# Expert weights as plain fp32 in column groups, instead of split in two fp32r parts

## The chip, the cores and the metric

The kernel runs on one core of one Trainium2 chip. The metric is the device time of one execution in microseconds (us); lower is better. A core has TensorE (PE, whose weight loads are listed as PEld), VectorE (DVE), ScalarE (ACT), GpSimd (POOL) and SyncE (SP, which here issues the loads). TensorE can be used as one array of 128 columns, or in column groups of 64 or 32, each with weights of its own and writing to its own partitions of PSUM.

## The reference

One step of a diffusion backbone of width 1024 with 128 context tokens and 512 latent tokens. After the attention part comes a layer of experts, on which the change works:

```
def expert_choice_ffn(h, w_router, w_gate, w_up, w_down):
    cap = CAPACITY_FACTOR * n // N_EXPERTS          # 64 latent, 16 context tokens for each of 16 experts
    aff = softmax(h @ w_router)
    gates, idx = top_k(swapaxes(aff, 1, 2), cap)
    xe = h[idx]
    a = einsum('becd,edf->becf', xe, w_gate)        # 1024 x 1024 per expert, fp32
    u = einsum('becd,edf->becf', xe, w_up)
    ye = einsum('becf,efd->becd', silu(a) * u, w_down) * gates
    return zeros.at[idx].add(ye)                    # added to the chosen tokens' rows
...
x = x + gate2 * expert_choice_ffn(h, *moe_w)        # then a last RMSNorm
```

Context tokens and latent tokens choose separately, with the same weights. All inputs are fp32.

## The kernel before

The first 600 us are projections and attention; their code doesn't change. Then the layer of experts runs in four groups of four experts. An expert has three weights (gate, up, down; `BLOCK_ORDER` interleaves them so that a hidden row is ready when "down" needs it), and each weight comes in 8 halves of 128 x 1024 fp32, 512 KB: 96 halves a group, 384 in all. SP issues one DMA a half into one of `ESLOT` = 12 slots, once PE has counted (`s_half`) that the slot's last half is used.

A half is split before use: ScalarE writes `w_hi` (the weight rounded to fp32r, L1608), VectorE the rest, `raw_lo` or `extra_lo` (L1972), four halves ahead (`LEAD`). The tokens are split in the same way (`xe_hi`, `xe_lo`; hidden rows `ht2_hi`, `ht2_lo`). The tokens are the stationary operand: 80 columns, 64 latent and 16 context. `half_product` (L1238) makes, for each side of 512 columns, three fp32r products (hi x hi, hi x lo, lo x hi; L1246 to L1248). The result stands on partitions 0 to 79 of two banks.

Between the halves PE does three more things. `turn_hidden` (L1230) transposes the hidden rows of an expert (8 transposes), at the third and fourth half of the next gate block. `find_rows` (L1208, L1210) looks up the chosen tokens' row numbers and gates for four experts, once a group: plain fp32 products with 64 columns (latents) and 16 columns (context, from partition 64). `gather` and `gather_context` (L1193, L1177) pick the next group's tokens by products with a 0/1 matrix, in the last "down" block of a group. `spare` (L1237) and `keep_warm` (L1156) are fillers. `gate_spread` (L1130, L1132) puts the second gate's row onto the partitions ahead of the experts.

After "down", VectorE multiplies by gate and modulation (`y_g`), and GpSimd adds the 80 rows of 4 KB to `x1_dram` by an indirect DMA (`scatter`, L2433), one after the other. The last expert isn't scattered: its eight "down" halves run one side first (all of side 0, then the end of side 1), VectorE adds `y_g` to gathered rows, and two indirect DMAs write them to the outputs (L2449, L2451).

Each engine's work is an order written out by hand; semaphores alone tie them. A plain fp32 product appears in the trace as two records (and two weight loads), an fp32r product as one.

Of the kernel before, what the change touches and what calls it, by code (L numbers as in the profile page):

```python
# [51 lines left out]
ESLOT, LEAD = 12, 4  # L52
# [137 lines left out]
T_ID, T_IOTA, T_SLAT, T_SCTX, T_EPS, T_NH, T_ONES = 0, 128, 192, 193, 194, 195, 196  # L190
T_KEPT = 200
# [5 lines left out]
def table_of_constants():  # L197
# [9 lines left out]
    t[:, T_ONES] = 1.0  # L207

# [18 lines left out]
def build(nc, x_prompt, x_sample, cache_attn_k, cache_attn_v, cache_diff_k, cache_diff_v, c, c_ctx,  # L227
# [5 lines left out]
    with ctx:  # L233
# [25 lines left out]
        gate_e = sb("gate_e", [P, EG])  # L259
        rows_e = sb("rows_e", [P, NE], U32)  # L260
# [104 lines left out]
        extra_lo = [at("extra_lo0", 129024, [P, 2, HALF], F32R), at("extra_lo1", 88064, [P, 2, HALF], F32R)]  # L365
        ht2_hi = at("ht2_hi", 96256, [P, KD, EROWS], F32R)
        ht2_lo = at("ht2_lo", 100352, [P, KD, EROWS], F32R)
        h_act = at("h_act", 104448, [P, 2, NW])
        y_g = at("y_g", 108544, [P, 2, D])
        sel_c = at("sel_c", 151040, [P, EG * CAPC], F32R)  # L370
        sel_g = at("sel_g", 137216, [P, NTL, EG * CAPL], F32R)
        x_lat = at("x_lat", 141312, [P, 2, EG * CAPL])
# [8 lines left out]
        x1_dram = nc.dram_tensor("x1_dram", [TOK, D], F32).ap()  # L381
# [31 lines left out]
        s_gb1 = sem("s_gb1"); s_gb2 = sem("s_gb2"); s_xr = sem("s_xr")  # L413
# [6 lines left out]
        s_selg = sem("s_selg"); s_g = sem("s_g"); s_xeh = sem("s_xeh"); s_xel = sem("s_xel")  # L420
# [7 lines left out]
        s_out = sem("s_out"); s_kout = sem("s_kout"); s_htf = sem("s_htf"); s_kn = sem("s_kn"); s_xet = sem("s_xet")  # L428
        s_q2 = [sem("s_q2a"), sem("s_q2b")]; s_yme = sem("s_yme"); s_xech = sem("s_xech"); 
# [69 lines left out]
        def expert_half(h):  # L499
            s = h % ESLOT  # L500
            return raw_half(raw, DENSE_HALVES + s) if s < 2 * NRAW else extra[(s - 2 * NRAW) // 2][:, s % 2, :]

        def expert_lo_half(h):
            s = h % ESLOT
            return raw_half(raw_lo, DENSE_HALVES + s) if s < 2 * NRAW else extra_lo[(s - 2 * NRAW) // 2][:, s % 2, :]
# [60 lines left out]

        def latent_slots(xe, k):
            return xe[:, k, :].rearrange("p (e s) -> p e s", s=EROWS)[:, :, 0:CAPL]

        def by_expert(x):  # L570
            return x.rearrange("p (e s) -> p e s", s=CAPL)

        def context_slots(xe):
            return xe.rearrange("p k (e s) -> p (k e) s", s=EROWS)[:, :, CAPL:EROWS]

        def hidden_bank(f):
            return bank(6 + f).rearrange("p (k c) -> p k c", c=P)[:, :, 0:EROWS]
# [35 lines left out]
        def _(sp):  # L613
# [58 lines left out]
            def body(i, first):  # L672
                for h in range(GH):
# [4 lines left out]
                    if first and h == 8:  # L678
                        for t in range(NT):
                            sp.wait_ge(s_x1, t + 1)  # L680
                            sp.dma_start(x1_dram[t * P:(t + 1) * P, :], x_r[:, t, :]).then_inc(s_x1out, 16)
                    if not first or h >= ESLOT:
# [4 lines left out]
                    elif h == 2 * NRAW:  # L687
                        sp.wait_ge(s_lgt, 2)
                    elif h == 2 * NRAW + 2:
                        sp.wait_ge(s_xl, NT)  # L690
# [6 lines left out]
            sp.wait_ge(s_scat, 16 * (NE - 1))  # L697
# [12 lines left out]
        def _(pe):  # L710
# [411 lines left out]
            def gate_spread(r):  # L1122

                pe.wait_ge(s_grow, r + 1)
                if r == 0:
                    pe.wait_ge(s_gb2, 16)
                b = 6 + r
                for v in range(2):
# [3 lines left out]
                pe.matmul(bank(b), ones_m[0:1, :], gate2[0:1, r * NW:(r + 1) * NW], start=False, stop=True)\  # L1132
                  .then_inc(s_post, 1)
# [64 lines left out]
            def find_rows(i, first, last):  # L1198
# [4 lines left out]
                if not first:  # L1203
                    pe.wait_ge(s_h2l, i * 8)
# [1280 lines left out]
```

## Time and profile before

| | us |
|---|---|
| median of 3 runs | 1240.54 |
| lowest, highest | 1237.38, 1240.97 |
| span of the profiled execution | 1235.4 (its time around the span is not given) |
| busy PE, weight loads | 1191.7, 859.5 |
| busy DVE, ACT, POOL | 913.9, 721.9, 181.6 |
| bytes moved | 291.62 MB, mean 236 GB/s |

The profile's page gives busy time by engine, the chain that ended last and the costliest lines; the stage tables and timelines are answers of the trace to a question about a stretch. Durations of matmuls overlap: what a matmul costs is the distance to the next one's start, not its own length. The layer of experts lies between about 613 and 1221 us, 384 x 512 KB = 201 MB of the bytes.

### The profile page before, as it was taken

Reading aid. Unit: us, or ns where it says so; the run is one execution under the profiler, and the core shown is the slowest. Engines: PE = TensorE matmul, PEld = TensorE weight load, DVE = VectorE, ACT = ScalarE, POOL = GpSimd, SP = SyncE. Lnnn points to the kernel's source line nnn. Section 1 sums busy time; section 2 is a strip of 40 time slices with the busy share of each in tenths; the row PEclk is TensorE's granted clock in tenths of the full one; section 3 lists DMA queues with packets and bytes.
Section 4 is the critical chain, followed back from the end, with each engine's and each line's share of the span. In section 5 each row is a group of like instructions: output and inputs, shape, how many; then the busy total and the mean of one; then the engine's idle time right before and its main releaser. Section 6 shows DMA issues by size and latency. Waiting matters only on the chain.

```text
span 1235.4 us, 17478 instructions
## 1 busy us (share of the span) xinstructions
PE 1191.7 (96%) x6111; PEld 859.5 (70%) x6111; DVE 913.9 (74%) x1145; ACT 721.9 (58%) x1029; POOL 181.6 (15%) x154
## 2 busy tenths in 40 slices
PE   6999999999999999999899999999999999999994
PEld 4778877788777777778476667666676666766662
DVE  3673658899682322444778999899997999979995
ACT  4432357777641230223567776788766777667774
POOL 1344330000000000100400111110114110111220
PEclk9999999999999999999889999999999999999997
DMA  9932250110424444472559998899989999799995
GB/s 361 332 134 69 71 117 23 44 31 14 184 68 171 136 136 145 155 265 70 220 187 330 387 376 306 314 373 386 384 268 321 369 387 385 257 335 366 380 392 196
DMA packets 110862, 291.62 MB, mean 236 GB/s; under 512 B 29265, under 2 KB 30498, under 8 KB 110274
## 3 DMA queue, kind: packets, MB, share of 16 engines
q1 hardware_dynamic: 106576, 273.16, 60.8%
q0 software_dynamic: 3792, 12.86, 4.2%
q10 hardware_dynamic: 418, 4.63, 1.0%
q8 instruction: 43, 0.70, 0.2%
q14 instruction: 33, 0.27, 0.1%
HBM read 269.64 MB, written 15.73 MB: 231 GB/s over the span
## 4 chain that ended last, share of the span: by engine, by line
PE 87%; DVE 6%; ACT 3%; issue 2%; DMA 1%; ACTq 0%; POOL 0%; DVEq 0%; POOLq 0%
PE ps L1246 14%; PE ps L1247 14%; PE ps L1248 14%; PE ps L742 9%; PE ps L743 8%; PE ps L744 8%; PE ps L968 2%; PE ps L952 2%; DVE neg_max L1881 2%; PE ps L1193 1%; PE ps L991 1%; PE ps L1194 1%; PE ps L987 1%; DVE q_lo_t L1873 1%; PE ps L764 1%
## 5 line engine op out<-in xcount | busy, mean ns | idle before, releaser
L1972 DVE TENSOR_TENSOR raw_lo<-raw,w_hi 128x1024 fp32r<-128x1024 f32 x256 | 304.6, 1218 | 44.9 <-ACT w_hi L1608 33.4
L1608 ACT ACTIVATE w_hi<-raw 128x1024 fp32r<-128x1024 f32 x252 | 264.8, 1060 | 79.7 <-PE ps L1248 79.7
L1246 PE MATMUL ps<-w_hi,xe_hi 128*80 128x512 f32 x512 | 204.6, 400 | 0.0
L1248 PE MATMUL ps<-w_hi,xe_lo 128*80 128x512 f32 x512 | 203.3, 397 | 0.0
L2433 POOL DMA_INDIRECT x_dram<-y_g,rows_e x15 | 93.6, 6238 | 499.6 <-DVE y_g L2201 499.6
L1972 DVE TENSOR_TENSOR extra_lo<-extra,w_hi 128x1024 fp32r<-128x1024 f32 x128 | 152.6, 1219 | 7.0 <-ACT w_hi L1608 5.9
L1608 ACT ACTIVATE w_hi<-extra 128x1024 fp32r<-128x1024 f32 x128 | 135.9, 1064 | 36.6 <-PE ps L1248 36.6
L742 PE MATMUL ps<-w_hi,ht 128*128 128x512 f32 (+1 forms) x320 | 124.8, 390 | 0.0
L744 PE MATMUL ps<-w_hi,ht 128*128 128x512 f32 (+1 forms) x320 | 121.7, 380 | 0.0
L743 PE MATMUL ps<-raw_lo,ht 128*128 128x512 f32 (+1 forms) x320 | 121.7, 380 | 0.0
L522 DVE TENSOR_TENSOR raw_lo<-raw,w_hi 128x1024 fp32r<-128x1024 f32 x48 | 57.6, 1225 | 78.9 <-ACT w_hi L517 78.3
L517 ACT ACTIVATE w_hi<-raw 128x1024 fp32r<-128x1024 f32 x48 | 48.8, 1053 | 114.2 <-DMA raw<-in_w_in_dram 66.3
L1247 PE MATMUL ps<-raw_lo,xe_hi 128*80 128x512 f32 x288 | 114.1, 396 | 0.0
L1248 PEld LDWEIGHTS ps<-w_hi,xe_lo 128*80 128x80 f32 x512 | 76.5, 149 | 43.5 <-issue 1.4
L1246 PEld LDWEIGHTS ps<-w_hi,xe_hi 128*80 128x80 f32 x512 | 76.7, 150 | 40.8 <-issue 1.4
L1246 PE MATMUL ps<-w_hi,ht_hi 128*80 128x512 f32 x256 | 100.9, 394 | 0.3 <-DVE ht_lo L2190 0.2
L1248 PE MATMUL ps<-w_hi,ht_lo 128*80 128x512 f32 x256 | 100.6, 393 | 0.0
L1247 PE MATMUL ps<-extra_lo,xe_hi 128*80 128x512 f32 x224 | 89.0, 397 | 0.0
L1247 PE MATMUL ps<-raw_lo,ht_hi 128*80 128x512 f32 x224 | 88.2, 394 | 0.0
L742 PEld LDWEIGHTS ps<-w_hi,ht 128*128 128x128 f32 x320 | 60.1, 188 | 16.6 <-issue 5.2
L744 PEld LDWEIGHTS ps<-w_hi,ht 128*128 128x128 f32 x320 | 60.0, 187 | 12.9
L743 PEld LDWEIGHTS ps<-raw_lo,ht 128*128 128x128 f32 x320 | 60.1, 188 | 11.2
(328 smaller groups left out, 2056.4 us busy)
## 6 DMA issues: line engine op xcount, KB each, us to landing
raw<-in_w_exp_down_dram SPq DMA_DIRECT2D x112, 512.0 KB, 6.4
raw<-in_w_exp_gate_dram SPq DMA_DIRECT2D x80, 512.0 KB, 5.4
extra<-in_w_exp_up_dram SPq DMA_DIRECT2D x64, 512.0 KB, 5.6
raw<-in_w_exp_up_dram SPq DMA_DIRECT2D x64, 512.0 KB, 5.5
extra<-in_w_exp_gate_dram SPq DMA_DIRECT2D x48, 512.0 KB, 5.2
raw<-in_w_in_dram SPq DMA_DIRECT2D x16, 1024.0 KB, 5.7
raw<-in_w_mod_dram SPq DMA_DIRECT2D x12, 1024.0 KB, 7.1
raw<-in_w_mod_dram SPq DMA_DIRECT2D x16, 512.0 KB, 11.0
```

The lines of the kernel that those rows point to most:

```text
L517: act.activation(w_hi[:, n % NHL, :], raw_half(raw, h), ACT.Copy).then_inc(s_hi, 1)
L522: dve.tensor_tensor(raw_half(raw_lo, h), raw_half(raw, h), w_hi[:, n % NHL, :].bitcast(F32), ALU.subtract)\
L742: pe.matmul(b, stat_hi(k, tt), hi[:, kk, :], start=first, stop=False)
L743: pe.matmul(b, stat_hi(k, tt), lo[:, kk, :], start=False, stop=False)
L744: mm = pe.matmul(b, stat_lo(k, tt), hi[:, kk, :], start=False, stop=last)
L952: mm = pe.matmul(bank(bb, 0, n), q[:, m % 4, t * P:(t + 1) * P], keys_t[:, x, c0:c0 + n], start=(part == 0), stop=(part == 1))
L1246: pe.matmul(b, stat_hi, hi[:, cols], start=(k == 0), stop=False)
L1247: pe.matmul(b, stat_hi, lo[:, cols], start=False, stop=False)
L1248: mm = pe.matmul(b, stat_lo, hi[:, cols], start=False, stop=(k == KD - 1))
L1608: act.activation(w_hi[:, (DENSE_SPLITS + h) % NHL, :], expert_half(h), ACT.Copy)\
L1972: dve.tensor_tensor(expert_lo_half(h), expert_half(h), w_hi[:, (DENSE_SPLITS + h) % NHL, :].bitcast(F32), ALU.subtract).then_inc(s_lo, 1)
L2433: pool.indirect_dma_start(x1_dram[:, :], bass.IndirectOffsetOnAxis(ap=rows_e[0:EROWS, n:n + 1], axis=0), y_g[0:EROWS, n % 2, :], None, com ...
```

## The change

- The weights aren't split. A half is used as it landed, as plain fp32; the tokens too (`xe_l` latents, `xe_c` context padded to 32, `ht2_l`, `ht2_c`). The split instructions of ScalarE and VectorE in this stage go, and `half_product` waits for the slot's DMA.
- `half_product` makes two products of 64 stationary columns (latents) over 512 columns each, in column groups 0 to 63 and 64 to 127 of one bank, and four of 32 (context) over 256 columns each in four groups of the next. A side of the result thus stands on other partitions: latents in half rows, context in quarter rows.
- The last expert's eight halves (`side_product`) put, for each side, latents on partitions 0 to 63 and context on 64 to 95.
- The hidden rows are turned by four transposes (`turn_latents`) and two (`turn_context`) of 128 columns.
- `find_rows` puts each table on both 64-partition groups and on four 32-partition groups; `gate_spread` makes the gate's rows in those layouts as well; row numbers are doubled or quadrupled.
- `scatter` issues two indirect DMAs for an expert, 128 half rows of 2 KB and 128 quarter rows of 1 KB; the padding goes to 16 spare rows behind `x1_dram`, which SP fills with one more store.
- Sixteen slots: the room of `w_hi` becomes `extra_ring`.

```
-ESLOT, LEAD = 12, 4
+ESLOT = 16
...
-        xe_hi = at("xe_hi", 61440, [P, KD, EG * EROWS], F32R)
-        xe_lo = at("xe_lo", 74752, [P, KD, EG * EROWS], F32R)
+        xe_l = at("xe_l", 61440, [P, KD, EG * CAPL])
+        xe_c = at("xe_c", 69632, [P, KD, EG, 32])
...
-                def half_product(h, banks, stat_hi, stat_lo, k, sides=(0, 1)):
-                    pe.wait_ge(s_lo, i * GH + DENSE_SPLITS + h + 1)
-                    hi, lo = w_hi[:, (DENSE_SPLITS + h) % NHL, :], expert_lo_half(h)
-                    for f in sides:
-                        cols = slice(f * NW, (f + 1) * NW)
-                        b = bank(banks + f, rows=slice(0, EROWS))
-                        pe.matmul(b, stat_hi, hi[:, cols], start=(k == 0), stop=False)
-                        pe.matmul(b, stat_hi, lo[:, cols], start=False, stop=False)
-                        mm = pe.matmul(b, stat_lo, hi[:, cols], start=False, stop=(k == KD - 1))
-                    if 1 in sides:
+                def half_product(h, banks, latents, context, k):
+
+                    pe.wait_ge(s_slot[h % ESLOT], expert_raw(h, i))
+                    w, flags = expert_half(h), {"start": k == 0, "stop": k == KD - 1}
+                    for f in range(2):
+                        pe.matmul(bank(banks, rows=slice(64 * f, 64 * f + 64)), latents, w[:, f * NW:(f + 1) * NW], **flags)
+                    for q in range(4):
+                        mm = pe.matmul(bank(banks + 1, 0, 256, slice(32 * q, 32 * q + 32)), context,
+                                       w[:, 256 * q:256 * q + 256], **flags)
+                    mm.then_inc(s_half, 1)
+
+                def side_product(h, f, latents, context, k):
+
+                    pe.wait_ge(s_slot[h % ESLOT], expert_raw(h, i))
+                    w, flags = expert_half(h)[:, f * NW:(f + 1) * NW], {"start": k == 0, "stop": k == KD - 1}
+                    pe.matmul(bank(4 + f, rows=slice(0, CAPL)), latents, w, **flags)
+                    mm = pe.matmul(bank(4 + f, rows=slice(64, 96)), context, w, **flags)
+                    if f:
                         mm.then_inc(s_half, 1)
                     elif k == KD - 1:
                         mm.then_inc(s_front, 1)
...
                for e in range(EG):
                     cols = (e * (NE + 1), (e + 1) * (NE + 1))
                     for t in range(NTL):
+                        for f in range(2):
+                            pe.matmul(bank(6, *cols, slice(64 * f, 64 * f + 64)),
+                                      sel_g[:, t, e * CAPL:(e + 1) * CAPL].bitcast(F32), aff_n[:, t, :],
+                                      start=(t == 0), stop=(t == NTL - 1))
+                    cols = ((EG + e) * (NE + 1), (EG + e + 1) * (NE + 1))
+                    for g in range(4):
+                        mm = pe.matmul(bank(6, *cols, slice(32 * g, 32 * g + 32)), sel_c[:, e, :].bitcast(F32),
+                                       aff_n[:, NTL, :], start=True, stop=True)
...
-            def expert_lo(h, i):
-                dve.wait_ge(s_hi, i * GH + DENSE_SPLITS + h + 1)
-                dve.tensor_tensor(expert_lo_half(h), expert_half(h),
-                                  w_hi[:, (DENSE_SPLITS + h) % NHL, :].bitcast(F32), ALU.subtract).then_inc(s_lo, 1)
...
-                pool.indirect_dma_start(x1_dram[:, :], bass.IndirectOffsetOnAxis(ap=rows_e[0:EROWS, n:n + 1], axis=0),
-                                        y_g[0:EROWS, n % 2, :], None, compute_op=ALU.add).then_inc(s_scat, 16)
+                pool.indirect_dma_start(x1_halves[:, :], bass.IndirectOffsetOnAxis(ap=rows_l[:, n:n + 1], axis=0),
+                                        y_l[:, n % 2, :], None, compute_op=ALU.add).then_inc(s_scat, 16)
+                pool.indirect_dma_start(x1_quarters[:, :], bass.IndirectOffsetOnAxis(ap=rows_x[:, n:n + 1], axis=0),
+                                        y_c[:, n % 2, :], None, compute_op=ALU.add).then_inc(s_scat, 16)
```

TensorE's order before, in any block of the stage, here "down" (`ht_hi`, `ht_lo` are the hidden rows; 80x512 is stationary columns by streamed columns):

```order
L1246 MATMUL ps<-w_hi,ht_hi 80x512
L1247 MATMUL ps<-raw_lo,ht_hi 80x512
L1248 MATMUL ps<-w_hi,ht_lo 80x512
L1246 MATMUL ps<-w_hi,ht_hi 80x512
L1247 MATMUL ps<-extra_lo_133,ht_hi 80x512
L1248 MATMUL ps<-w_hi,ht_lo 80x512
```

And after the change, in the gate block of the second expert, with the transposes of the first expert's hidden rows (`h_l` latents, `h_c` context):

```order
L1278 MATMUL ps<-raw,xe_l 64x512 x2
L1280 MATMUL ps<-raw,xe_c 32x256 x4
L1257 MATMUL ps<-tab,h_l 128x128 x4
L1278 MATMUL ps<-raw,xe_l 64x512 x2
L1280 MATMUL ps<-raw,xe_c 32x256 x4
L1265 MATMUL ps<-tab,h_c 128x128 x2
L1278 MATMUL ps<-raw,xe_l 64x512 x2
L1280 MATMUL ps<-raw,xe_c 32x256 x4
```

Six products of one size a half have become two of 64 columns and four of 32, in turn; the transposes stand between halves as before. In the last expert's last block, after the change (L1271 are fillers):

```order
L1271 MATMUL ps<-sel_g 128x256 x9
L1257 MATMUL ps<-tab,h_l 128x128 x4
L1265 MATMUL ps<-tab,h_c 128x128 x2
L1271 MATMUL ps<-sel_g 128x256 x11
L1288 MATMUL ps<-extra_ring,ht_l 64x512
L1289 MATMUL ps<-extra_ring,ht_c 32x512
L1288 MATMUL ps<-extra_ring,ht_l 64x512
L1289 MATMUL ps<-extra_ring,ht_c 32x512
```

There a product of 64 columns and one of 32, both over 512 columns, follow each other 16 times.

## Rows read from the trace of the kernel before

**Rows 1.** The page's first lines: span, busy time by engine, share, instructions.

```profile
span 1235.4 us, 17478 instructions
PE 1191.7 (96%) x6111; PEld 859.5 (70%) x6111; DVE 913.9 (74%) x1145; ACT 721.9 (58%) x1029; POOL 181.6 (15%) x154
```

**Rows 2.** The chain that ended last, by line.

```profile
PE ps L1246 14%; PE ps L1247 14%; PE ps L1248 14%; PE ps L742 9%; PE ps L743 8%; PE ps L744 8%; PE ps L968 2%; PE ps L952 2%; DVE neg_max L1881 2%; PE ps L1193 1%; PE ps L991 1%; PE ps L1194 1%; PE ps L987 1%; DVE q_lo_t L1873 1%; PE ps L764 1%
```

**Rows 3.** Busy time by stage (stretch, length, engines, clock, DMA share, GB/s).

```profile
core 0: us, PE busy (x) PEld busy (x) DVE busy (x) ACT busy (x) POOL busy (x), PEclk, DMA share, GB/s
606.20:623.20 17.00, 16.77 (x58) 12.21 (x59) 11.81 (x29) 2.90 (x6) 2.32 (x2) 0.50 0.18 62
...
943.90:947.70 3.80, 3.80 (x12) 2.28 (x12) 1.37 (x4) 0.89 (x1) 2.50 (x1) 0.55 0.67 184
...
1150.00:1203.00 53.00, 53.00 (x236) 34.09 (x235) 48.89 (x45) 41.89 (x43) 14.05 (x3) 1.00 1.02 389
```

**Rows 4.** PE timeline, first matmuls of two blocks (start, length, idle before in brackets).

```profile
700.23 0.39 PE L1246 MATMUL ps<-w_hi,ht_hi 128*80 128x512 f32 x1
...
711.31 0.39 PE L1246 MATMUL ps<-w_hi,xe_hi 128*80 128x512 f32 x1
```

**Rows 5.** Chain in order of time: two look-ups of rows (start, length).

```profile
793.08 0.57 PE ps L1208 x8
...
941.21 0.57 PE ps L1208 x8
```

**Rows 6.** PE timeline, four column groups between 128-column products.

```profile
38.63 0.39 PE L896 MATMUL ps<-w_hi,ht 128*128 128x512 f32 x1
38.95 1.90 PE L774 MATMUL ps<-raw,vec_t 128*2 128x512 f32 x16
40.77 0.50 PE L894 MATMUL ps<-w_hi,ht 128*128 128x512 f32 x1
41.11 0.39 PE L895 MATMUL ps<-raw_first_lo,ht 128*128 128x512 f32 x1
```

**Rows 7.** PE timeline of two 64-column groups, and their line's durations.

```profile
191.63 1.52 PE L987 MATMUL ps<-p_t,va_n 128*64 128x256 f32 x12
193.07 0.77 PE L968 MATMUL ps<-tab,probs 128*128 128x128 f32 x5
...
L987 PE MATMUL ps<-p_t,va_n x192: 379/379/431, 191.6 to 265.4; 128*64 128x256 f32 x192
```

**Rows 8.** PE timeline of the look-up, 64 and 16 columns in turn, and L1208's durations.

```profile
643.43 0.64 PE L1208 MATMUL ps<-aff_n,sel_g 128*64 128x17 f32 x8
644.00 0.22 PE L1210 MATMUL ps<-aff_n,sel_c 128*16 128x17 f32 x2
644.15 0.64 PE L1208 MATMUL ps<-aff_n,sel_g 128*64 128x17 f32 x8
...
L1208 PE MATMUL ps<-aff_n,sel_g x128: 210/210/231, 643.4 to 1093.5; 128*64 128x17 f32 x128
```

**Rows 9.** PE timeline, transposes of the hidden rows.

```profile
692.76 0.44 PE L1230 MATMUL ps<-tab,h_act 80*128 80x80 f32 x4
693.00 0.44 PE L1246 MATMUL ps<-w_hi,xe_hi 128*80 128x512 f32 x1
```

**Rows 10.** PE timeline ahead of the experts.

```profile
603.75 0.73 PE L1156 MATMUL ps<-xn_hi 128*128 128x512 f32 x2
606.43 1.98 PE L1130 MATMUL ps<-mod_keep,tab 128*64 128x512 f32 x4 [1.95 <-ACT mod_keep L1590]
...
613.20 0.71 PE L1167 MATMUL ps<-tab,pos_t 16*128 16x16 f32 x5
```

**Rows 11.** The scatter's line: durations, first and last start.

```profile
L2433 POOL DMA_INDIRECT x_dram<-y_g,rows_e x15: 5537/5537/13485, 681.6 to 1194.5; - x15
```

**Rows 12.** Chain in order of time, the end.

```profile
1220.63 0.75 DVE y_g L2261
...
1227.04 0.30 POOL out_dram L2449
```

More of the change, by code:

```diff
@@ L190 @@
 T_ID, T_IOTA, T_SLAT, T_SCTX, T_EPS, T_NH, T_ONES = 0, 128, 192, 193, 194, 195, 196
+T_OFFL, T_OFFC = 197, 198
 T_KEPT = 200
@@ L207, in table_of_constants @@
     t[:, T_ONES] = 1.0
+    t[:, T_OFFL] = p // 64
+    t[:, T_OFFC] = np.where(p % 32 < CAPC, p // 32, 4 * (TOK + p % 32 - CAPC) + p // 32)
     for v in range(2):
@@ L1131, in gate_spread @@
                               start=True, stop=False)
-                pe.matmul(bank(b), ones_m[0:1, :], gate2[0:1, r * NW:(r + 1) * NW], start=False, stop=True)\
-                  .then_inc(s_post, 1)
+                bias = gate2[0:1, r * NW:(r + 1) * NW]
+                pe.matmul(bank(b), ones_m[0:1, :], bias, start=False, stop=True)
+                if r == 0:
+                    pe.wait_ge(s_affc, 1)
+                half = slice(64 * r, 64 * r + 64)
+                o = T_SB - T_KEPT
+                pe.matmul(bank(4, rows=half), tab2[:, o:o + 64], mod_keep[:, r, :], start=True, stop=False)
+                pe.matmul(bank(4, rows=half), ones_m[0:1, half], bias, start=False, stop=True)
+                for g in range(2):
+                    rows, cols = slice(64 * r + 32 * g, 64 * r + 32 * g + 32), slice(256 * g, 256 * g + 256)
+                    pe.matmul(bank(1, 0, 256, rows), tab2[:, o + P:o + P + 32], mod_keep[:, r, cols], start=True, stop=False)
+                    mm = pe.matmul(bank(1, 0, 256, rows), ones_m[0:1, rows], bias[:, cols], start=False, stop=True)
+                mm.then_inc(s_post, 1)
             for n in range(NT, 2 * NT):
@@ L1635, in body @@
                                 gathered(0, q, True)
-                        if not last or KD * n + k + LEAD < GH:
-                            expert_hi(KD * n + k + LEAD, i)
                         if before == "g" and k == 1:
@@ L1640, in body @@
                             silu(e1, 1)
-                        if before == "u" and kind == "g" and k in (4, 5):
-                            hidden_hi(e1, k - 4)
+                        if before == "u" and kind == "g" and k == 4:
+                            latents_turned(e1)
                         if (kind, e) == ("d", EG - 1):
@@ L2208, in body @@
                         h = KD * n + k
-                        if first and n == 0:
-                            for q in GATHERS_READ.get(k, ()):
-                                gathered(0, q, True)
                         if before == "u" and k == 0:
@@ L2217, in body @@
                             output(e1)
-                        if not last or h + LEAD < GH:
-                            expert_lo(h + LEAD, i)
                         if before == "d" and k == 1 and (n or not first) and not early:
                             output(e1)
-                        if before == "u" and kind == "g" and k in (4, 5):
-                            hidden_lo(e1, k - 4)
+                        if before == "u" and kind == "g" and k == 5:
+                            context_turned(e1)
                         if h == 12:
```

328 lines of the change are left out of this document (163 added, 165 removed).

## The prediction, written before the change was run

> **What bounds the kernel now.** I read the page's busy shares first. TensorE (PE) is busy 96% of a span of 1235.4 us [rows 1]. A busy PE need not be PE at its peak, so the chain of waits comes next: the three matmul lines of the expert stage, L1246 to L1248, hold 42% of it, and VectorE 6% [rows 2]. The stage table then says what runs beside them: in a full stretch of experts PE has no gap, VectorE is at 48.89 of 53 us, ScalarE at 41.89, the DMA share is 1.02 and 389 GB/s move at full clock [rows 3]. So PE sets the pace of the 384 weight halves (16 experts, 3 matrices, 8 halves of 512 KB), the splits on ScalarE and VectorE fit under it, and the transfers have little room: 524,288 B at 389 GB/s are 1.35 us a half. The PE timeline gives the pace: a block of 8 halves starts at 700.23 and the next at 711.31, so a half costs 11.08 / 8 = 1.385 us for 6 matmuls, 0.231 each [rows 4]. A whole group of four experts, from one look-up of rows to the next, takes 941.21 - 793.08 = 148.1 us [rows 5].
>
> **The change, part by part: the pace of a half.** The splits go away, which frees VectorE and ScalarE but nothing on the path. What counts is PE's new work for a half: two plain fp32 products over 512 columns in column groups of 64, then four over 256 columns in groups of 32. The trace has plain fp32 products in groups. A plain fp32 product leaves two records. L774's 16 records are 8 products in four groups, four rounds; they start at 38.95 and the next line at 40.77 [rows 6]. So a round over 512 columns is under (40.77 - 38.95) / 4 = 0.455 us, and 0.43 once the end is taken off (below). L987's 12 records are six rounds of two 64-wide groups over 256 columns: 193.07 - 191.63 = 1.44 us, 0.216 a round plus what the ends cost [rows 7]. Groups of one size thus run side by side. Streams of a half: 2 x 0.43 + 2 x 0.216 = 1.29 us, 0.09 less than now.
>
> Against it stands the end of each such run. From the last fp32r matmul at 38.63 to L774 at 38.95 pass 0.32 us where the pitch is 0.231: 0.09 lost. L774's own 1.82 us are 4 x 0.427 (two passes over 512 columns need 1024 / 2.4 GHz) and 0.11 lost, and the L894 behind shows 0.50 where its neighbours show 0.39: its 128-column load is exposed, 0.11 [rows 6]. L987 loses 1.44 - 6 x 0.216 - 0.05 = 0.10, where 0.05 is its own first load (maximum 431 ns against a median of 379) [rows 7]. The look-up of rows changes from 64-wide to 16-wide groups and back for each expert: a record more costs (0.64 - 0.21) / 7 = 0.06, but 8 records and the change take 0.57 and 2 records and the change back 0.15, which leaves 0.09 and up to 0.10 or 0.13 (the second run's records may overlap) [rows 8]. The two groups lie on different columns, and no wait is named between them. The transposes L1230 between 128-wide matmuls take 0.24 + 0.05 for four, no such loss [rows 9]. So what costs 0.1 us is a change of group size, not of line or data. The new half changes size twice: 2 x 0.10, and the first load of each run, 0.05 for 64 columns [rows 7] and about 0.02 for 32 (an estimate between nothing and that). Half: 1.29 + 0.20 + 0.07 = 1.56; I take 1.57, as four groups start a little apart. Ends: 1.47 (0.09 a change, loads hidden) and 1.71 (0.13 a change, loads of 0.05 and 0.11).
>
> The Trainium skill, TensorEngine Tiling (Array Packing), Key Properties, says that a change of tiling mode, and not one of tile alone, drains the array; it gives no price. By it both changes of a half are drained, also where 64- and 32-wide groups share columns, which no row here has.
>
> 376 halves run so (all but the last eight): 376 x (1.57 - 1.385) = +69.6 us; ends +32 and +122.
>
> **The last eight halves.** They go side by side: for each half and side one 64-wide product over 512 columns, then one 32-wide, on other columns but of another size, as in rows 8. Each pays both changes: 0.86 + 0.10 + 0.02 + 0.86 + 0.11 + 0.05 = 1.98 us (rounded up by a hundredth, less for an even start), 16 times, 31.7 us for 8 x 1.385 = 11.1: +20.6. Ends +19 and +23.
>
> **Transposes, gathers, look-up.** Before, eight transposes of an expert cost 2 x 0.29 [rows 9]. Now they are four and two of 128 columns instead of 80, 0.24 / 4 x 128 / 80 = 0.10 each, and each of the two runs breaks in between 32- and 64-wide groups: one change more, with a load of 0.11. 6 x 0.10 + 2 x 0.21 = 1.02, less 0.58: +0.44, 16 times, +7. The gathers that stand between halves add one change each in the same way: about 19 of them at 0.21, +4. The look-up puts its 64-wide records in pairs of groups, so 16 take the time of 8, and its four 32-wide ones run beside each other: nothing, but 0.8 for the extra table of the last group. Sum +11.8; ends +7 and +16.
>
> **The gate rows before the experts.** gate_spread runs twice and gets two 64-wide and four 32-wide products more each: 2 x 0.86 + 2 x 0.43 + changes, 3.2 us at full clock, 5.6 to 6.2 at half. The first stands before an idle of 1.95 us, the second before fillers that wait for the positions at 613.20 [rows 10]. In this stretch the clock is at its lower level, 1.2 GHz, from 606.2 to 623.2 [rows 3], after PE had idled. If the new work fills that idle, the gathers behind run at 2.4 GHz and up to 4 us come back; if not, up to 7 are lost. I take +2. Two fills with zeros on VectorE stand there too, about 1 us beside the same wait.
>
> **Scatter and tail.** Two scatters of 128 pieces for one of 80 rows: GpSimd takes 5.5 us now (median) [rows 11]; 2 x 5.5 x 128 / 80 = 18 us, and an expert lasts over 35: hidden. After the last y at 1220.63 the chain goes through a tile of x_f whose output ends just before GpSimd's scatter at 1227.04 [rows 12]. With ScalarE and VectorE free that tile is out long before; the last rows themselves could be scattered about 2 us earlier: -2. The sixteen slots and the transfers cost nothing at 1.57 us a half (334 GB/s): the DMA share falls.
>
> **Sum.** 1235.4 + 69.6 + 20.6 + 11.8 + 2 - 2 = 1337.4 us of span. The profile gives no time of its execution beside the span; the runs' median, 1240.54, lies 5.1 above it (the fastest run 2.0), so 1342.5 us.
>
> **Rivals.** (a) The changes of size inside a half are free, since both sizes use the same columns or the loads slip in ahead. Then a half is 1.29. In a group PE takes 96 x 1.29 = 124 us and the transfers 96 x 1.35 = 130; the gathers give the transfers some 10 us more and sixteen slots carry it over, so PE leads: 376 x -0.095 = -36, the last block 8 x (1.72 - 1.385) = +2.7, transposes 16 x (0.64 - 0.58) = +1, the look-up +1, tail -2: 1202 of span, 1207 us. If the transfers lead, -13 instead, 1230. For it: no row changes size on the same columns. Against it: every change in the trace costs the same 0.1, also between columns that don't touch. It wins from a change below 0.04 us on. Chance 9%.
> (b) Only one of the two directions costs. Half 1.43: +17, last block +18, rest +11: 1286. Against it: rows 6 and 8 show both directions. 5%.
> (c) The groups don't run side by side with 64 and 32 wide weights: 2 x 0.86 + 4 x 0.43 = 3.44 us, +790 us, 2030. Rows 6 and 7 speak against it; 1%. The Trainium skill, TensorE: Matmul & The Clock Gate, Part 3, measured 2.38 times from three 32-wide groups, not 3; by that the streams would be 1.29 / 0.79 = 1.63, a half 1.90 and the time about 1467. The four groups of rows 6 don't show it.
> (d) The change costs more than I say: clock drops like the one behind the look-up (a mean of 0.55 over 3.8 us, 1.7 lost [rows 3]) come at other places too, because the array streams 82% of a half instead of 92%, or loads are exposed at each round. 1380 and more, 6%. Against it: the full stretch of experts in rows 3 stands at 1.00, transposes included.
>
> **Numbers.** My case 79%, with its own range of 1298 to 1375. The range for 8 in 10 is 1293 to 1382: it takes in the one-change case only at its edge. What can be told from no change is 0.3%, 3.7 us. Faster 9% (a), same 1%, slower 90%.
>
> **What would show it.** In the profile after: a gap of about 0.1 us before the first load of each run of two and of four; a half every 1.57 us; a group in about 169.5 us; the last eight halves in some 32 us; DMA share near 0.85 and under 340 GB/s in full stretches; ScalarE and VectorE under a fifth busy in them. I am wrong if halves come every 1.3 us, or if the waits of PE name slots (DMA).

## The result, and the profile after

The changed kernel takes 1348.98 us (median of 4 runs, 1342.0 to 1353.77) where the kernel before takes 1239.43 (4 runs, 1237.38 to 1240.97). The ratio is 1.0882, 95% interval 1.0842 to 1.0922: slower, by 109.6 us. Forecast were 1342.5 us, between 1293 and 1382. The profiled execution took 1352.62 us, with a span of 1350.8. Ratios here and below leave out an execution more than 1.5% above the fastest of its kernel; there was one, the 1255.47 us of the kernel with all groups 32 wide.

The first lines and the chain of waits by line, to be read against [rows 1, 2]:

```profile
span 1350.8 us, 20882 instructions
PE 1308.1 (97%) x8618; PEld 662.1 (49%) x8618; DVE 425.2 (31%) x704; ACT 317.6 (24%) x627; POOL 135.3 (10%) x169
PE ps L1278 28%; PE ps L1280 16%; PE ps L747 8%; PE ps L748 8%; PE ps L749 8%; PE ps L973 2%; DVE neg_max L1912 2%; PE ps L957 2%; PE ps L1211 1%; PE ps L996 1%; PE ps L1288 1%; PE ps L1212 1%; PE ps L1289 1%; DMA raw_first<-in_w_in_dram 1%; DVE q_lo_t L1904 1%
```

VectorE has lost 489 us of work and ScalarE 404, and the kernel got slower: almost none of it stood on the path (at the very end some did, see the tail below). The two lines of the new half, L1278 (latents) and L1280 (context), hold 44% of the chain where three lines held 42%.

The stage table, for [rows 3] (stretch, length, busy time and count by engine, clock, DMA share, GB/s). The first row is the stretch ahead of the experts, the others lie in them:

```profile
607.50:634.80 27.30, 27.30 (x71) 12.31 (x71) 10.94 (x26) 3.08 (x7) 2.72 (x2) 0.50 0.17 61
700.00:800.00 100.00, 100.00 (x764) 28.94 (x766) 9.38 (x20) 6.25 (x12) 8.77 (x6) 1.00 0.92 320
800.00:900.00 100.00, 100.00 (x832) 27.75 (x836) 7.20 (x19) 5.51 (x11) 6.21 (x4) 1.00 0.89 305
1000.00:1100.00 100.00, 100.00 (x834) 25.82 (x826) 8.64 (x22) 3.54 (x7) 6.21 (x4) 1.00 0.93 326
```

PE has no gap and full clock; VectorE and ScalarE are under a tenth busy; the DMA share went from 1.02 to about 0.9. The PE timeline of two halves shows the new pace, for [rows 4] (start, length, line, stationary columns, streamed columns, records):

```profile
1295.48 1.08 PE L1278 MATMUL ps<-raw,xe_l 128*64 128x512 f32 x4
1296.49 0.64 PE L1280 MATMUL ps<-raw,xe_c 128*32 128x256 f32 x8
1297.06 1.08 PE L1278 MATMUL ps<-raw,xe_l 128*64 128x512 f32 x4
1298.07 0.64 PE L1280 MATMUL ps<-raw,xe_c 128*32 128x256 f32 x8
```

A half is 1297.06 - 1295.48 = 1.58 us: 1.01 for the latents and 0.57 for the context. Streams alone (the time in which the columns pass through the array) would be 0.86 and 0.43. The starts of the look-ups, for [rows 5]:

```profile
658.94 0.65 PE L1227 MATMUL ps<-aff_n,sel_g 128*64 128x17 f32 x16
829.19 0.65 PE L1227 MATMUL ps<-aff_n,sel_g 128*64 128x17 f32 x16
1001.93 0.65 PE L1227 MATMUL ps<-aff_n,sel_g 128*64 128x17 f32 x16
1170.59 0.65 PE L1227 MATMUL ps<-aff_n,sel_g 128*64 128x17 f32 x16
```

With them the 115.4 us of added span are divided. Before, the first look-up starts at 643.43 [rows 8]: up to it +15.5 us. The three groups from there on take 170.25, 172.74 and 168.66 us where 149.6, 148.1 and 149.8 stood. The first of them holds a short stretch at the lower clock behind its look-up, after as before. The second of them holds a pause of TensorE that the kernel before doesn't have. The chain names it "issue", that is, no semaphore:

```profile
980.56 2.46 issue
983.02 1.98 PE ps L1278 x4
```

Behind it the granted clock is 0.50 from 983.0 to 986.4, so the latents of the next half take 1.98 us and not 1.01. The pause thus costs 2.46 us and the clock behind it 1.6 more: 172.74 against the 168.66 of a group without either.

### The profile page after: what moved, and what is told of

Read it like the earlier page. It is cut to its first block, busy times and chain, and to the rows that moved or that the text cites. A ratio compares the mean times of both kernels' runs of the same rounds, so it can differ in the third digit from the quotient of the medians.

```text
span 1350.8 us, 20882 instructions
## 1 busy us (share of the span) xinstructions
PE 1308.1 (97%) x8618; PEld 662.1 (49%) x8618; DVE 425.2 (31%) x704; ACT 317.6 (24%) x627; POOL 135.3 (10%) x169
## 4 chain that ended last, share of the span: by engine, by line
PE 87%; DVE 5%; DMA 3%; ACT 2%; issue 2%; SPq 1%; POOL 0%; ACTq 0%; DVEq 0%; POOLq 0%
PE ps L1278 28%; PE ps L1280 16%; PE ps L747 8%; PE ps L748 8%; PE ps L749 8%; PE ps L973 2%; DVE neg_max L1912 2%; PE ps L957 2%; PE ps L1211 1%; PE ps L996 1%; PE ps L1288 1%; PE ps L1212 1%; PE ps L1289 1%; DMA raw_first<-in_w_in_dram 1%; DVE q_lo_t L1904 1%
## 5 line engine op out<-in xcount | busy, mean ns | idle before, releaser
L1278 PE MATMUL ps<-raw,xe_l 128*64 128x512 f32 x640 | 173.7, 621 | 2.5 <-issue 2.5
L1280 PE MATMUL ps<-raw,xe_c 128*32 128x256 f32 x1280 | 102.7, 393 | 0.0
L1280 PEld LDWEIGHTS ps<-raw,xe_c 128*32 128x32 f32 x1280 | 25.2, 108 | 130.8 <-issue 130.8
L536 DVE TENSOR_TENSOR raw_lo<-raw,w_hi 128x1024 fp32r<-128x1024 f32 x48 | 57.7, 1226 | 78.9 <-ACT w_hi L531 78.3
L531 ACT ACTIVATE w_hi<-raw 128x1024 fp32r<-128x1024 f32 x48 | 48.8, 1052 | 116.5 <-DMA raw<-in_w_in_dram 68.0
L1278 PEld LDWEIGHTS ps<-raw,xe_l 128*64 128x64 f32 x640 | 31.8, 135 | 63.8 <-issue 63.3
L1912 DVE TENSOR_REDUCE neg_max<-ps 128x1 f32<-128x768 f32 x64 | 58.2, 951 | 2.5 <-PE ps L957 2.3
L1278 PE MATMUL ps<-extra_ring,xe_l 128*64 128x512 f32 x192 | 53.5, 636 | 0.0
L1278 PE MATMUL ps<-extra,xe_l 128*64 128x512 f32 x192 | 52.2, 622 | 0.0
L1278 PE MATMUL ps<-extra_ring,ht_l 128*64 128x512 f32 x176 | 47.5, 618 | 0.0
L1278 PE MATMUL ps<-extra,ht_l 128*64 128x512 f32 x176 | 47.5, 618 | 0.0
```

The costliest lines, as they stand in the source:

```text
L531: act.activation(w_hi[:, n % NHL, :], raw_half(raw, h), ACT.Copy).then_inc(s_hi, 1)
L536: dve.tensor_tensor(raw_half(raw_lo, h), raw_half(raw, h), w_hi[:, n % NHL, :].bitcast(F32), ALU.subtract)\
L1278: pe.matmul(bank(banks, rows=slice(64 * f, 64 * f + 64)), latents, w[:, f * NW:(f + 1) * NW], **flags)
L1280: mm = pe.matmul(bank(banks + 1, 0, 256, slice(32 * q, 32 * q + 32)), context, w[:, 256 * q:256 * q + 256], **flags)
L1912: dve.tensor_reduce(nm, src[:, :, 0:384], AX.XY, ALU.max, negate=True).then_inc(s_max, 1)
```

## Experiments

Each kernel has its own median and that of the kernel before on the same chip; the changed kernel was run ahead of all of them (kernel before: 1239.43 us). Medians of the kernel before differ by up to 1.7 us between these sessions, so smaller differences across them say nothing. The first four were run together (kernel before: 1238.16 us, 13 runs).

**One change of size a half.** Every second half takes the context first, so that two halves of one kind of product follow each other.

```
-for f in range(2): latents ...
-for q in range(4): context ...
+order = (of_latents, of_context) if h % 2 == 0 else (of_context, of_latents)
+order[0]()
+order[1]().then_inc(s_half, 1)
```

> Every second half takes its context products first, so a half changes group size once instead of twice; products, loads and transfers stay. Theory (a change of group size costs 0.1 us and an exposed first load): a half falls from 1.58 to 1.43 us, 376 x -0.145 = -54, given back in part because transposes and gathers between halves now add two changes instead of one, +7: about 1302 us. Rival (the 0.28 us a half come from the number of products and loads, or from waits on slots): unchanged, 1349.

Measured: 1301.15 us (1294.38 to 1301.93, 4 runs), ratio 1.0491 (1.0460 to 1.0522); 47.8 us less than the changed kernel, as expected. The PE timeline of this kernel:

```profile
860.08 1.94 PE L1279 MATMUL ps<-extra_ring,xe_l 128*64 128x512 f32 x8
861.95 0.64 PE L1285 MATMUL ps<-extra_ring,xe_c 128*32 128x256 f32 x8
```

Two halves' latents take 861.95 - 860.08 = 1.87 us, where one half's took 1.01. With 0.86 of streams each, a run of latents loses 0.15 whether it is one half long or two. The cost hangs on the change, not on the products: their number is the same.

**No change of size in a half.** The latents too go in groups of 32: four products of 32 columns over 512 in place of two of 64. The same streams, no other edit.

```
-for f in range(2):
-    pe.matmul(bank(banks, rows=slice(64 * f, 64 * f + 64)), latents, w[:, f * NW:(f + 1) * NW], **flags)
+for q in range(4):
+    f, part = q // 2, 32 * (q % 2)
+    pe.matmul(bank(banks, rows=slice(32 * q, 32 * q + 32)), latents[:, part:part + 32],
+              w[:, f * NW:(f + 1) * NW], **flags)
```

> Latents too in groups of 32: four products of 32 columns over 512 instead of two of 64, the same result on the same partitions; no change of size within a half, more products (8 instead of 6). Theory: a half falls to 1.30 us, -104 us, +6 for transposes and gathers that now add two changes: about 1251 us if PE leads, up to 1270 if the transfers (1.35 us a half) do. Rival (number of products and loads sets the pace): slower than 1349. The last block is unchanged, 31.7 us.

Measured: 1240.13 us (1234.87 to 1255.47, 10 runs), ratio 1.0030 (0.9997 to 1.0062): nearly the whole loss is gone. Some rows of its timeline and its stage table:

```profile
859.88 1.04 PE L1279 MATMUL ps<-extra_ring,xe_l 128*32 128x512 f32 x8
860.73 0.61 PE L1282 MATMUL ps<-extra_ring,xe_c 128*32 128x256 f32 x8
861.16 1.04 PE L1279 MATMUL ps<-extra,xe_l 128*32 128x512 f32 x8
...
800.00:900.00 100.00, 100.00 (x1211) 40.71 (x1203) 10.26 (x22) 4.41 (x9) 9.32 (x6) 1.00 1.03 388
```

A half is 1.28 to 1.29 us, 0.85 and 0.43: the streams and nothing else, though it has eight products where six were. Nor does it lose anything between 512 and 256 streamed columns or from one bank to the next, so neither is what costs time in the changed kernel. In the stage of experts TensorE still waits for no transfer, at 388 GB/s.

376 halves at 0.29 less are 109 us. That the medians differ by 108.9 is partly chance. The two profiled spans are 112.3 us apart, and some 7 of these don't come from halves: the positions come 4.7 us earlier (622.35 for 627.05, below), a stretch of low clock behind the first look-up (1.6 us) is missing, and the pause with what follows it is 0.7 shorter. The 105 that are left are the 109 less what the transposes and gathers now lose, since each of them stands between two changes where it added one. The time came 11 us below the expectation, which had counted with a half of 1.30 and with the changed kernel's start.

**The last eight halves in 32-wide groups.** Otherwise the changed kernel.

```
-pe.matmul(bank(4 + f, rows=slice(0, CAPL)), latents, w, **flags)
+for part in (0, 32):
+    pe.matmul(bank(4 + f, rows=slice(part, part + 32)), latents[:, part:part + 32], w, **flags)
```

> Only the last expert's eight down halves: latents as two groups of 32 beside the context's 32, so three groups of one size run side by side. Theory: two streams of 0.86 us a half, 8 x 1.72 = 13.8 instead of 31.7 us: about -18, 1331 us. Rival (the last block is hidden beside the end's loads and norms, or groups of 64 and 32 ran beside each other already): within 4 us of 1349.

Measured: 1326.34 us (1321.72 to 1335.25, 4 runs), ratio 1.0737 (1.0686 to 1.0788), 22.6 less. In the changed kernel and in this one the last block begins and ends so:

```profile
1303.44 1.07 PE L1288 MATMUL ps<-extra_ring,ht_l 128*64 128x512 f32 x2
...
1335.20 0.75 DVE L2270 SCALAR_TENSOR_TENSOR y_z<-ps,gate_z,gate 80x512 f32<-80x512 f32 x1 [5.05 <-PE ps L1289]
```

```profile
1290.31 0.62 PE L1289 MATMUL ps<-extra_ring,ht_l 128*32 128x512 f32 x2
...
1304.30 0.75 DVE L2271 SCALAR_TENSOR_TENSOR y_z<-ps,gate_z,gate 80x512 f32<-80x512 f32 x1 [0.57 <-PE ps L1290]
```

31.8 us against 14.0: 17.8 of the gain are here. The rest lies ahead of the experts, in code that this edit doesn't touch and that differs from execution to execution, as the next experiment shows.

**Gate rows later.** The added products of the gate's layouts, six for each half of the gate's row and twelve in all, no longer stand between `gate_spread` and the positions, where each pair worked from `mod_keep` and the bias. Six in all, from the finished gate row, stand before the first "up" block.

```
-pe.matmul(bank(4, rows=half), tab2[...], mod_keep[:, r, :], start=True, stop=False)
-pe.matmul(bank(4, rows=half), ones_m[0:1, half], bias, start=False, stop=True)
-for g in range(2): ... two products each into bank 1
+def gate_layouts():
+    pe.wait_ge(s_gate2, 2)
+    for r in range(2): pe.matmul(bank(4, rows=half), ones_l[0:1, half], gate2[0:1, ...])
+    for g in range(4): mm = pe.matmul(bank(5, 0, 256, rows), ones_l[64:65, rows], gate2[64:65, ...])
...
+if first and (kind, e) == ("u", 0): gate_layouts()
```

> The gate rows for the new layouts are made behind the first gate block, at full clock, from the finished gate row (2 products of 64 columns and 4 of 32, from one row each), instead of 12 products ahead of the experts at half clock. Theory (this was the mis-sized term, +12 us where +2 was forecast): the first gather starts about 12 us earlier, 1.5 us are paid later: about 1338 us. Rival (the stretch waits for the positions or the gate row anyway): unchanged, 1349.

Measured: 1340.13 us (1339.25 to 1343.31, 4 runs), ratio 1.0830 (1.0810 to 1.0850), 8.9 less, and the spread of the runs is 4 us in place of 12. By the ratios alone the gain isn't clear of the noise, as their intervals overlap; the timelines carry it. The PE timeline of the changed kernel, from the second gate row to the positions:

```profile
612.53 1.98 PE L1135 MATMUL ps<-mod_keep,tab 128*64 128x512 f32 x4
614.44 2.07 PE L1138 MATMUL ps<-gate,ones_m 1*128 1x512 f32 x2
616.44 1.97 PE L1144 MATMUL ps<-mod_keep,tab 128*64 128x512 f32 x2
618.34 1.97 PE L1145 MATMUL ps<-gate,ones_m 1*64 1x512 f32 x2
...
624.20 2.93 PE L1173 MATMUL ps<-xn_hi 128*128 128x512 f32 x6
627.05 0.71 PE L1184 MATMUL ps<-tab,pos_t 16*128 16x16 f32 x5
```

and of this one:

```profile
608.82 1.98 PE L1136 MATMUL ps<-mod_keep,tab 128*64 128x512 f32 x4 [1.95 <-ACT mod_keep L1636]
610.73 2.07 PE L1139 MATMUL ps<-gate,ones_m 1*128 1x512 f32 x2
612.73 2.93 PE L1174 MATMUL ps<-xn_hi 128*128 128x512 f32 x6
615.59 0.71 PE L1185 MATMUL ps<-tab,pos_t 16*128 16x16 f32 x5
```

The added rows of the second gate half run from 616.44 to 624.20, 7.8 us, because a product over 512 columns takes 1.9 us there and not 0.95 or 1.0. The positions come at 615.59 in place of 627.05. How dear it gets differs from execution to execution: the kernel with the last block in groups of 32 has the very same products here, and in its profiled execution it ran them at full clock, in 4.2 us:

```profile
612.24 1.07 PE L1144 MATMUL ps<-mod_keep,tab 128*64 128x512 f32 x2
...
616.42 1.65 PE L1173 MATMUL ps<-xn_hi 128*128 128x512 f32 x6
618.01 0.48 PE L1184 MATMUL ps<-tab,pos_t 16*128 16x16 f32 x5
```

Four executions with these products have the positions at 618.01, 622.35, 627.05 and 627.82; the granted clock from 606.2 to 640 was 0.95, 0.90, 0.60 and 0.70. The seven profiled executions of the kernels below and of this one, all without them, have the positions between 615.12 and 617.96.

**All three.** The 32-wide half, the 32-wide last block and the late gate rows together. It, the next kernel and one with twelve slots were run together (kernel before: 1237.69 us, 9 runs).

> The three edits together: latents in groups of 32 everywhere, the last block in three groups of 32, the gate rows made later. Theory (the causes are separate and add up on PE): 1240 - 18 to 23 for the last block - 9 for the gate rows: 1208 to 1213 us, 2.5% below the kernel before. Rival (with PE at 1.29 us a half the transfers, 1.35 us a half at 389 GB/s, lead and swallow it): 1225 us or more, with waits of PE on DMA.

Measured: 1221.01 us (1219.49 to 1222.24, 4 runs), ratio 0.9861 (0.9846 to 0.9876): 1.4% faster than the kernel before, clear of the noise, and so faster than both. It lies 8 to 13 us above the sum of the single gains. Those had counted the start twice: the all-32 kernel's profiled execution had its first look-up at 649.92 already, against 658.94, and the combined one has it at 647.83. From there to the last matmul the two take 572.4 and 556.4 us, 16.0 apart: the 17.8 of the last block less 1.8 that the group with the pause takes more (147.7 for 146.0).

**Fewer changes, shorter look-up.** From that kernel, both sets of transposes stand behind one half, and the look-up of rows goes in 32-wide groups as well.

> e5 with the remaining changes of size thinned out: latent and context transposes of an expert behind one half instead of two, and the look-up of rows in groups of 32 throughout. Theory: a pair of changes less for 15 experts (0.3 us each, -5) and for each look-up (0.24 us times 16, -4): 9 us below e5, near 1201 us. Rival (PE no longer leads): the same as e5.

The edits are those of the two kernels that follow, in one.

Measured: 1219.17 us (1218.46 to 1222.59, 5 runs), ratio 0.9855 (0.9842 to 0.9869). Some 9 us were expected and 1.8 came. So the two edits were run apart, below.

**Twelve slots.** `ESLOT = 12`, otherwise the combined kernel.

> e5 with twelve slots instead of sixteen. At 1.29 us a half PE asks for 406 GB/s in a block, the rows of before show 389 at most; in a group the transfers fall 96 x 0.06 = 6 us behind and catch up in the gathers. Theory: twelve slots (15 us of PE's work, of which a transfer's way takes 5) still cover that: within 3 us of e5. Rival (the sixteen slots are what keeps PE fed at this pace): slower than e5 by 5 to 20 us, with waits on DMA.

Measured: 1221.47 us (1218.64 to 1223.0, 4 runs), ratio 0.9863 (0.9848 to 0.9878), no difference that the runs can tell. The four slots are worth nothing at this pace.

**The transposes alone** (run with the next two; kernel before: 1238.18 us, 7 runs).

```
-if kind == "g" and e and k == 2:
-    turn_latents(e - 1)
 if kind == "g" and e and k == 3:
+    turn_latents(e - 1)
     turn_context(e - 1)
```

> The kernel with all products 32 wide, three groups in the last block and late gate rows (1221.0 us, span 1220.4), with both sets of transposes behind the same half (four size changes fewer in each of the 12 places, some 0.05 to 0.2 us each time). The kernel that had this and a look-up in 32-wide groups came 1.8 us below and showed three new pauses of TensorE of 1.9, 2.0 and 4.1 us a little behind the look-ups, with 'issue' as what ended them. If these pauses come from the look-up's many short instructions (160 products in 1.38 us), they are not here: one pause of about 3.2 us stays, and the time is 1219 to 1221. If they come from the moved transposes, they are here, and the time is 1226 to 1228.

Measured: 1217.78 us (1214.17 to 1218.29, 4 runs), ratio 0.9824 (0.9796 to 0.9852). This is the lowest median here, a little under what was expected; its interval still overlaps that of the combined kernel. The timelines show the gain: a group takes 141.77 us for 142.63, that is 0.29 for each of the three places where the transposes stood apart, the price of a pair of changes again.

**The look-up alone.**

```
-for f in range(2):
-    pe.matmul(bank(6, *cols, slice(64 * f, 64 * f + 64)), sel_g[:, t, e * CAPL:(e + 1) * CAPL] ...)
+for q in range(4):
+    part = e * CAPL + 32 * (q % 2)
+    pe.matmul(bank(6, *cols, slice(32 * q, 32 * q + 32)), sel_g[:, t, part:part + 32] ...)
```

> The same kernel with the look-up in 32-wide groups alone (160 products and 160 loads where 96 were; each of the four look-ups takes 1.38 us where 2.93 were, 6.2 us less in all). If short instructions run the supply dry, the pauses of 1.9, 2.0 and 4.1 us behind the look-ups are here, 6 to 8 us in all beside the one of 3.2, and the time is 1220 to 1222, no gain. If the pauses come from the moved transposes, they are gone, and the time is 1214 to 1215.

Measured: 1224.24 us (1223.47 to 1225.08, 4 runs), ratio 0.9888 (0.9864 to 0.9913): no faster than the combined kernel without it (1221.01, with overlapping intervals) and 2 us above the expectation, though the look-ups themselves got shorter. The waits of PE (line, what ended them, us in all, times, longest), first with the look-up changed, then with the transposes:

```profile
PE ps L1241 <- issue: 4.3, 1, 4.3
PE ps L1281 <- issue: 3.1, 1, 3.1
PE ps L1284 <- issue: 2.7, 2, 1.6
PE ps L1229 <- issue: 0.9, 1, 0.9
```

```profile
PE ps L1280 <- issue: 2.9, 1, 2.9
```

The pause of about 3 us is in both; the others are in the first kernel and not in the second, one within the first look-up (L1229), one within the last (L1241), and two (L1284) 5.0 us behind the start of the second and third. They take 7.9 us, where the shorter look-ups (1.35 us in place of 2.95) would save 6.4 in all. The kernel with both edits has three of them, and no kernel with the old look-up has one as long, beside the one at the jump. TensorE starts a record of these products every 10 ns or so, and no semaphore is awaited when it stops. That it had run ahead of its supply of instructions fits these rows; the kernels don't show it directly. The Trainium skill, Runtime: NRT & Kernel Launch, Instruction fetch mechanics, bears on both kinds of pause. It says that a taken branch stalls the engine when its target lies outside the pages of instructions that it holds. The pause that every profiled kernel on the new code has comes once, where the loop over the two middle groups jumps back; the trace's record of that branch takes 4.18 us in the changed kernel and 0.23 in the one before, and the pause is 2.3 to 3.3 us wherever TensorE leads. Between two such records lie 2,751 records of matmuls and weight loads in the changed kernel and 1,587 in the one before; no run varies this length alone, so why the jump was free before stays open. The page also says that the fetch of straight code is hidden, because instructions are issued more slowly than they arrive. If these pauses are waits for instructions, the rows speak against it.

**How far behind are the transfers?** The context products of six halves in eight are left out, so the experts' context rows lack most of their sum. The weights still move.

```
-for q in range(4):
+for q in range(4 if k in (0, KD - 1) else 0):
```

> The same kernel with the context products of a half left out except in the first and last half of a block (so the experts' context rows are wrong): 6 of 8 halves take 0.86 us of TensorE in place of 1.29, the weights come as before. It asks how far the transfers are behind TensorE. If TensorE led with the transfers just keeping up (the windows show a share of 1.0 at 388 GB/s, no wait of TensorE on a transfer), the time falls only until the transfers lead: 384 halves of 0.524 MB at 388 to 399 GB/s take 505 to 519 us, and with the gathers' and scatters' 18 MB 45 us more, against 556 now: 1185, between 1170 and 1210, and TensorE waits on the rings' slots. If the transfers had already set the pace, it stays at 1219 to 1221. If they have room to spare, it goes with TensorE to some 1100.

Measured: 1176.55 us (1174.09 to 1177.6, 4 runs), ratio 0.9495 (0.9469 to 0.9521). Its waits of PE and a stretch of its stage table:

```profile
PE ps L1280 <- DMA raw<-in_w_exp_up_dram: 13.2, 27, 1.4
PE ps L1280 <- DMA extra<-in_w_exp_up_dram: 9.7, 16, 1.4
...
700.00:800.00 100.00, 92.47 (x926) 34.31 (x922) 9.60 (x21) 8.81 (x17) 9.74 (x7) 1.00 1.04 397
```

Here the transfers lead, at 394 to 397 GB/s. The time fell as expected and stopped where the transfers lead. So the combined kernels stand about 40 us above the floor of the transfers: TensorE still sets the end. Rival (a)'s milder form, in which the transfers take over at 1230, is refuted, by this kernel and by the 32-wide half, which comes every 1.29 us and waits for no transfer; they would take over near 1177.

## Why the prediction held, step by step

**The pace of a half: right.** 1.57 us were forecast and 1.58 came. The two kernels with half of the changes or none price it: a change with its first load costs 0.15 and 0.14 us in the two directions, 0.29 a half where 0.27 was the sum. The decisive choice was to read [rows 6 to 8] as the price of a change of size and to apply it where both sizes use the same columns, which no row showed. The Trainium skill, TensorEngine Tiling (Array Packing), Key Properties, says that a change of mode drains the array. The runs agree that a change costs time and give the price; that it is spent on draining they don't show. Streams of 1.29 us, with four groups of 32 fully side by side, are shown by the kernel without changes: rival (c) is refuted, the rate of 2.38 doesn't hold for these products, and (b) is refuted as well, since both directions cost.

**The last eight halves: right.** 1.98 us were forecast for each half and side, 31.7 in all (the terms as written add up to 2.00, or 32.0), and 1335.20 - 1303.44 = 31.8 came.

**Transposes, gathers, look-up: right in sum.** The groups grew by 20.6 us (first to second look-up, from 149.6 us by the timelines), where 17.8 of halves and about 3 of these were forecast. As a half grew by 0.195 and not 0.185, the halves took 18.7 of it, so these terms together are about 1 us a group too high.

**The gate rows ahead of the experts: the mis-sized term.** I took +2 within -4 to +7, expecting the new products to fill an idle after which the clock would come back. In the profiled execution the idle was filled and the clock stayed at its lower level for 27.3 us, against 17 before [rows 3], and the positions came 13.85 us later than 613.20 [rows 10]. The rows divide this:

```profile
605.45 1.07 PE L1144 MATMUL ps<-mod_keep,tab 128*64 128x512 f32 x2
...
611.38 1.22 PE L1173 MATMUL ps<-xn_hi 128*128 128x512 f32 x2
```

The first set of added products takes 5.9 us, from 605.45 to 611.38, and the second 7.8 [616.44 to 624.20, above]; 1.5 us of idle and fillers go, and everything starts 1.7 us later already (603.39 for 601.69), for a reason that I didn't look for. The fillers behind the second set take 2.9 us as before, and the way from the positions to the first look-up grows only by 1.7 (31.9 for 30.2), less than the 3.1 of its sixteen halves. So what was mis-sized is the price of the products themselves: at full clock a set takes 4.2 us where 3.2 were forecast, and at the lower level 7.8 where 5.6 to 6.2 were. I had counted the four 32-wide products as two side by side and two more. They go one after another, 0.99 us apart at the lower level (620.24, 621.23, 622.22, 623.21). The two of a pair add to one sum in one group, which explains half of this; why the pairs don't overlap stays open. And I had expected the filled idle to bring the clock back.

With the clock up, +2 is about right (it comes to 1 or 2): in the kernel with the last block in groups of 32, whose code is the same up to there, the first look-up starts at 648.22, 4.8 us later than before, of which 3 to 4 belong to halves and gathers. With the clock down the term is near 12. The four executions of the changed kernel show both: 1342.0 and 1345.35 us at a mean granted clock of 0.989 and 0.988, 1352.62 and 1353.77 at 0.980 and 0.982.

**The tail: about the size, by another way.** -2 was forecast, because the last tile of `x_f` would be out long before. It isn't. It still stands behind the last `y`, and from there to the end pass 1350.8 - 1335.20 = 15.6 us, where 14.8 passed [rows 1, 12]:

```profile
1334.12 1.05 PE L1289 MATMUL ps<-extra,ht_c 128*32 128x512 f32 x2
...
1335.98 0.69 DVE L2274 TENSOR_TENSOR x_l<-x_l,y_z 80x512 f32<-80x512 f32 x1
...
1336.78 1.28 DVE L2259 SCALAR_TENSOR_TENSOR x_f<-x_f,rs,g_fin 128x1024 f32<-128x1024 f32 x1
...
1341.55 0.95 POOL L2460 DMA_INDIRECT out_dram<-x_l,rows_z  x1 [44.61 <-DMA out_dram<-x_f]
```

VectorE's order is written out, and it puts the norm of that tile (L2259) behind the last `x_l` however free the engine is; GpSimd then waits 44.61 us for the tile's output. A free engine doesn't move what its own queue holds back. But the free VectorE helped one step earlier. Before, the last matmul ended at 1218.17 and the last `y` started 2.5 us later [rows 12], as VectorE still had the first side's rows and a norm to do:

```profile
1217.77 0.40 PE L1248 MATMUL ps<-w_hi,ht_lo 128*80 128x512 f32 x1
...
1219.43 1.28 DVE L2249 SCALAR_TENSOR_TENSOR x_f<-x_f,rs,g_fin 128x1024 f32<-128x1024 f32 x1
```

Now `y` starts 0.03 us behind it. From the last matmul's end to the end of the span pass 15.6 us where 17.2 passed: 1.6 came back.

**From the span to the time.** I put 5.1 us between them, from the median. Most of that isn't what lies around a span, which is 1352.62 - 1350.8 = 1.8 us after and 1.8 to 3.1 in later runs of the kernel before. The profiled execution before was a fast one (with 1.8 to 3.1 around it, its span gives 1237.2 to 1238.5, below the median of 1240.54), and the one after is 3.6 us above its median. So the spans overstate the change: 102.0 us were forecast, 115.4 came in the spans and 109.6 in the medians. Of the 13.4 between the spans and the forecast, some 10 are ahead of the first look-up and 2.5 are the pause at the loop's jump, which I had no term for; about 1 is in the last group and the tail.

How near 1342.5 is to 1348.98 is in part luck. The gate term alone differs by some 10 us from execution to execution, and the pace of a half, 0.01 us too low (3.8 us in all), and the transposes and gathers, some 4 us too high, cancel. What isn't luck is the growth of the 376 halves, +69.6 forecast and 73 measured.

**Rival (a), freed of its premise.** A half without the price of changes was put at 1.29 us and the kernel at 1207. That half was reached with other products, and the kernel with it, the short last block and late gate rows takes 1221, and 1217.78 with the transposes together. The rival had left out that the transposes and gathers then stand between two changes each: its group would take 148.1 - 96 x 0.095 = 139.0 us, and 142.6 were measured.

## What to carry to other kernels

Price what stands between instructions of unlike form, not only the instructions: 0.14 to 0.15 us a change was 109 us over 376 halves, more than the splits' relief could be worth, since these had been hidden. If an array is used in groups, try one group size for everything that alternates, and cut the wider operand to it: here eight products of one size beat six of two. Count products as side by side only where a row shows the same kind side by side. And before you free an engine or add slots, ask whether the end of anything waits for it.

## What the runs showed of the hardware

- A change between groups of 64 and of 32 columns costs 0.14 to 0.15 us in either direction, also where both use the same columns: a half of 1.58 us with two changes, 1.29 with none.
- Two 32-wide groups in place of one 64-wide cost no time: the latents take 0.85 us in four groups (x8 records), and 1.01 in two (x4), of which 0.86 are streams and the rest the change.
- An indirect scatter of 128 pieces of 2 KB takes GpSimd 1.55 us, not the 5.5 us of 80 pieces of 4 KB [rows 11], nor the 9 us each that I had scaled from these; 128 pieces of 1 KB take 1.55 us too. So the time doesn't go with the number of pieces alone:

```profile
L2442 POOL DMA_INDIRECT x_dram<-y_l,rows_l x15: 1546/1553/1743, 699.3 to 1289.2; - x15
```

- Many very short products in a row come with pauses of TensorE of 0.9 to 4.3 us that no semaphore explains, 7.9 us in all, enough to take back what look-ups of 1.35 us in place of 2.95 save.
- The loop's jump back costs TensorE a pause of 2.3 to 3.3 us with the new, longer loop body, and none before.
- The same products ahead of the experts ran at the lower or the higher clock level in different executions of the same code, with up to 10 us between them. What decides it stays open. With that work moved out of the stretch the runs of a kernel spread by 1.6 to 4.4 us, where they had spread by 8 to 21.
